# Fourier position transform split into even and odd parts, in a two-layer diffusion backbone on one core

## The reference, cut to what matters

```python
def fourier_mix(u, w_four):
    bn, length = u.shape[:2]
    ug = u.astype(jnp.float32).reshape(bn, length, C_GROUPS, C_GROUP_DIM)
    f = jnp.fft.fft2(ug, axes=(1, 3), norm='ortho').real.astype(u.dtype)
    return jnp.einsum('blgc,gcd->blgd', f, w_four).reshape(bn, length, C_WIDTH)

o = jnp.concatenate([window_attention_latent(...), global_attention_latent(...),
                     fourier_mix(uf, p['w_four'])], axis=-1) @ p['w_out']
h = h + g2 * o
```

## Time and profile before

| | us |
|---|---|
| median of 3 runs | 2835.33 |
| the profiled execution, as timed | 2834.34 |
| its span, first to last instruction | 2832.6 |
| PE busy | 2723.1 (96%) |
| DVE busy | 1471.4 (52%) |
| ACT busy | 981.8 (35%) |
| POOL busy | 767.5 (27%) |

### The profile page before, as it was taken

How to read it: one execution, slowest core, us unless ns; L and a number is a source line. 1 busy time by engine, 2 the same in 40 slices (tenths; PEclk the granted TensorE clock), 3 DMA queues, 4 the chain that set the end, 5 groups by cost and what they waited for, 6 DMA issues and landing times.

```text
span 2832.6 us, 37039 instructions
## 1 busy us (share of the span) xinstructions
PE 2723.1 (96%) x15204; PEld 2325.5 (82%) x15204; DVE 1471.4 (52%) x1926; ACT 981.8 (35%) x1503; POOL 767.5 (27%) x570
## 2 busy tenths in 40 slices
PE   6999999999988999999999999999999998999998
PEld 2888888888776888888888888888887777888887
DVE  1656655645288455565552555654225477433333
ACT  2433233324267243333331433332223366422232
POOL 1223422323167312343221132431011256100001
PEclk8999999999999999999999999999999999999999
DMA  5333333313411123333321233332212520233232
GB/s 222 101 108 124 120 103 112 111 54 138 134 36 37 38 100 109 113 127 106 113 91 60 86 113 123 126 97 78 68 59 94 160 60 1 82 97 104 89 99 81
DMA packets 70584, 274.36 MB, mean 97 GB/s; under 512 B 8720, under 2 KB 12048, under 8 KB 69392
## 3 DMA queue, kind: packets, MB, share of 16 engines
q1 hardware_dynamic: 70416, 271.99, 30.0%
HBM read 258.85 MB, written 13.11 MB: 96 GB/s over the span
## 4 chain that ended last, share of the span: by engine, by line
PE 84%; POOL 6%; DVE 4%; issue 2%; ACT 2%; DMA 1%; SPq 1%; POOLq 0%; DVEq 0%; ACTq 0%
PE ring L1337 72%; PE ring L1346 6%; POOL prob L518 4%; PE row L1187 1%; DVE wlo L932 1%; POOL xl L506 1%; PE ring L1296 1%; PE row L1444 1%; DMA q<-qk_parts 1%; ACT whi L609 1%; DVE t L1025 1%; DVE xl L1031 1%; PE row L1261 0%; PE bank L1422 0%; POOL xh L502 0%
## 5 line engine op out<-in xcount | busy, mean ns | idle before, releaser
L1337 PE MATMUL ring<-xh,whi 128*128 128x512 f32 (+1 forms) x2712 | 754.0, 346 | 10.6 <-DVE wlo L932 7.0
L1337 PE MATMUL ring<-xh,wlo 128*128 128x512 f32 (+1 forms) x2712 | 750.4, 345 | 0.0
L1337 PE MATMUL ring<-xl,whi 128*128 128x512 f32 (+1 forms) x2712 | 750.3, 345 | 0.0
L932 DVE TENSOR_TENSOR wlo<-raw,whi 128x1024 fp32r<-128x1024 f32 (+1 forms) x280 | 389.5, 1391 | 507.1 <-ACT whi L609 506.5
L462 POOL TENSOR_TENSOR ada_acc<-ada_acc,ada_tmp 128x384 f32<-128x384 f32 x252 | 335.2, 1330 | 601.7 <-ACT ada_tmp L621 581.0
L1337 PEld LDWEIGHTS ring<-xh,whi 128*128 128x128 f32 x2712 | 428.5, 188 | 77.1 <-issue 8.6
L1337 PEld LDWEIGHTS ring<-xh,wlo 128*128 128x128 f32 x2712 | 428.8, 188 | 66.2
L1337 PEld LDWEIGHTS ring<-xl,whi 128*128 128x128 f32 x2712 | 428.5, 188 | 65.4
L609 ACT ACTIVATE whi<-raw 128x1024 fp32r<-128x1024 f32 (+1 forms) x280 | 314.5, 1123 | 195.2 <-PE ring L1337 185.7
L949 DVE SCALAR_TENSOR_TENSOR ada_acc<-ada_buf,scond,ada_acc 128x384 f32<-128x384 f32 x294 | 353.6, 1203 | 6.9
L1337 PE MATMUL ring<-ah,whi 128*128 128x512 f32 (+1 forms) x1078 | 299.3, 347 | 0.0
(11 more groups left out here) (152 smaller groups left out, 2990.5 us busy)
## 6 DMA issues: line engine op xcount, KB each, us to landing
raw<-w_gu SPq DMA_DIRECT2D x176, 512.0 KB, 3.5
ada_buf<-w_ada SPq DMA_DIRECT2D x84, 768.0 KB, 4.2
raw<-w_down SPq DMA_DIRECT2D x64, 704.0 KB, 4.0
raw<-w_in SPq DMA_DIRECT2D x24, 512.0 KB, 3.6
ada_first<-w_ada SPq DMA_DIRECT2D x6, 1536.0 KB, 10.5
raw<-w_out SPq DMA_DIRECT2D x16, 512.0 KB, 3.7
k<-qk_parts SPq DMA_DIRECT2D x16, 384.0 KB, 6.7
q<-qk_parts SPq DMA_DIRECT2D x8, 576.0 KB, 9.8
```

The lines of the kernel that those rows point to most:

```text
L932: dve.tensor_tensor(wlo[:, slot, 0:nk * P], raw[:, slot, 0:nk * P], whi[:, slot, 0:nk * P].bitcast(F32), ALU.subtract).then_inc(wlo_ready, 1)
L1337: last = pe.matmul(out[:, a:b], w, x[:, k, a:b], start=(i == 0 and m == 0), stop=(i == nk - 1 and m == 2))
```

## The change

The position tables hold, per token block, 257 (129) cosine columns and 256 (128) sine columns, instead of 512 (256) of each. The cosine products go to one bank and the sine products to another. Chunk 0 uses `row[:, 0:512]` and `row[:, 512:1024]`; chunk 1 uses `row[:, 1024:1536]` and `bank[0]`, so it waits for nothing of chunk 0. ACT copies the odd part to `fodd` in SBUF. DVE forms the first half as even + odd, copies the middle column, and writes the second half mirrored as even - odd, into `fsum` in SBUF. ACT then rounds `fsum` into `xh` and DVE subtracts into `xl`. The transposes of tile 0 wait for `fsum_done` of chunk 1. The split of the second `w_out` tile moves from step 5 to the place behind the copies of `v1`. The rounding of chunk 1 moves to step 4 on ACT, and its rest to step 5 on DVE. The first write of ACT into the second half of `pth`, which lies over `fsum`, waits for that rest.

```diff
+        def fourier_banks(c):
+            return (row[:, 0:512], row[:, 512:1024]) if c == 0 else (row[:, 1024:1536], bank[0])
...
-        def act_fourier(act, layer):
+        def act_fourier(act, layer, between):
...
             for c in range(2):
                 wd = w_in_width(layer, UF[0])
+                odd, wo = fourier_banks(c)[1], (SEQ + CTX) // 2 if wd == TOK else SEQ // 2
+                if c == 0:
+                    between()
                 act.wait_ge(f2_done, 2 * layer + c + 1)
-                act.activation(xh[:, 6 + c, 0:wd], side[:, 0:wd], ACT.Copy).then_inc(fhi_done, 1)
+                act.activation(fodd[:, c, 0:wo], odd[:, 0:wo], ACT.Copy).then_inc(fodd_done, 1)
+                if c == 0:
+                    round_fourier(act, layer, 0)
+
+        def round_fourier(act, layer, c):
+            wd = w_in_width(layer, UF[0])
+            act.wait_ge(fsum_done, 2 * layer + c + 1)
+            act.activation(xh[:, 6 + c, 0:wd], fsum[:, c, 0:wd], ACT.Copy).then_inc(fhi_done, 1)
...
                         if i == 2:
-                            act_fourier(act, layer)
-                        if i == 5:
-                            split_hi(t + W_IN_TILES + 1, 1, KD)
+                            act_fourier(act, layer, lambda: split_hi(t + W_IN_TILES + 1, 1, KD))
+                        if i == 4:
+                            round_fourier(act, layer, 1)
...
+                            if j == 3:
+                                act.wait_ge(flo_done, 2 * layer + 2)
...
+            between()
             for c in range(2):
                 wd = w_in_width(layer, UF[0])
-                dve.wait_ge(fhi_done, 2 * layer + c + 1)
-                dve.tensor_tensor(xl[:, 6 + c, 0:wd], side[:, 0:wd], xh[:, 6 + c, 0:wd].bitcast(F32), ALU.subtract).then_inc(flo_done, 1)
+                dve.wait_ge(fodd_done, 2 * layer + c + 1)
+                even = fourier_banks(c)[0]
+                for n_, o, e0, o0 in ((SEQ, 0, 0, 0), (CTX, SEQ, SEQ // 2 + 1, SEQ // 2))[:2 if wd == TOK else 1]:
+                    hn = n_ // 2
+                    dve.tensor_tensor(fsum[:, c, o:o + hn], even[:, e0:e0 + hn], fodd[:, c, o0:o0 + hn], ALU.add)
+                    dve.tensor_copy(fsum[:, c, o + hn:o + hn + 1], even[:, e0 + hn:e0 + hn + 1])
+                    last = dve.tensor_tensor(fsum[:, c, o + n_ - 1:o + hn:-1], even[:, e0 + 1:e0 + hn], fodd[:, c, o0 + 1:o0 + hn], ALU.subtract)
+                last.then_inc(fsum_done, 1)
+                if c == 0:
+                    rest_of_fourier(dve, layer, 0)
...
                 if i == 2:
-                    dve_fourier(dve, layer)
+                    dve_fourier(dve, layer, lambda: split_lo(s["t"] + W_IN_TILES + 1, 1, KD))
                 if i == 5:
-                    split_lo(s["t"] + W_IN_TILES + 1, 1, KD)
+                    rest_of_fourier(dve, layer, 1)
...
-                    if c == 1:
-                        pe.wait_ge(flo_done, 2 * layer + 1)
-                    for tab, b0, nb, (lo, hi) in ((pos_lat, 0, 4, (0, SEQ)), (pos_ctx, 4, 2, (SEQ, TOK)))[:2 if blocks == 6 else 1]:
+                    even, odd = fourier_banks(c)
+                    for tab, n_, b0, e0, o0 in ((pos_lat, SEQ, 0, 0, 0), (pos_ctx, CTX, 4, SEQ // 2 + 1, SEQ // 2))[:2 if blocks == 6 else 1]:
+                        nb, hn = n_ // P, n_ // 2
                         for m in range(nb):
-                            for part in range(2):
-                                last = pe.matmul(side[:, lo:hi], v1[:, b0 + m, c, part * P:(part + 1) * P], tab[:, part, m],
-                                                 start=(m == 0 and part == 0), stop=(m == nb - 1 and part == 1))
+                            pe.matmul(even[:, e0:e0 + hn + 1], v1[:, b0 + m, c, 0:P], tab[:, m, 0:hn + 1], start=(m == 0), stop=(m == nb - 1))
+                        for m in range(nb):
+                            last = pe.matmul(odd[:, o0:o0 + hn], v1[:, b0 + m, c, P:2 * P], tab[:, m, hn + 1:n_ + 1], start=(m == 0), stop=(m == nb - 1))
...
-                    pe.wait_ge(flo_done, 2 * layer + 2)
+                    pe.wait_ge(fsum_done, 2 * layer + 2)
```

More of the change, by code:

```diff
@@ L226, in build @@
         uf = sb("uf", [P, 2, TOK], F32, work + 49152)
-        pos_lat = sb("pos_lat", [P, 2, 4, SEQ], F32, work + 55296)
-        pos_ctx = sb("pos_ctx", [P, 2, 2, CTX], F32, work + 71680)
+        pos_lat = sb("pos_lat", [P, 4, SEQ + 1], F32, work + 55296)
+        pos_ctx = sb("pos_ctx", [P, 2, CTX + 1], F32, work + 63520)
+        fsum = sb("fsum", [P, 2, TOK], F32, work + 65600)
+        fodd = sb("fodd", [P, 2, TOK // 2], F32, work + 71744)
         v1 = sb("v1", [P, 6, 2, 2 * P], F32, work + 75776)
@@ L274, in build @@
         f1_done, v1_even, v1_odd = sem("f1_done"), sem("v1_even"), sem("v1_odd")
-        f2_done = sem("f2_done")
+        f2_done, fodd_done, fsum_done = sem("f2_done"), sem("fodd_done"), sem("fsum_done")
         bn_done, bstd_done, brstd_done, unorm_done = sem("bn_done"), sem("bstd_done"), sem("brstd_done"), sem("unorm_done")
@@ L867, in dve_w_in, with dve_fourier @@
             rest_values(1)
-        def dve_fourier(dve, layer):
+        def dve_fourier(dve, layer, between):
             for blk in (1, 3, 5):
@@ L873, in dve_fourier, with rest_of_fourier @@
                 dve.tensor_copy(v1[:, blk].rearrange("p c n -> p (c n)"), bank[1][:, 0:4 * P]).then_inc(v1_odd, 1)
+            between()
             for c in range(2):
                 wd = w_in_width(layer, UF[0])
-                dve.wait_ge(fhi_done, 2 * layer + c + 1)
-                dve.tensor_tensor(xl[:, 6 + c, 0:wd], side[:, 0:wd], xh[:, 6 + c, 0:wd].bitcast(F32), ALU.subtract).then_inc(flo_done, 1)
+                dve.wait_ge(fodd_done, 2 * layer + c + 1)
[8 more added lines that the diff above has]
+                    rest_of_fourier(dve, layer, 0)
+        def rest_of_fourier(dve, layer, c):
+            wd = w_in_width(layer, UF[0])
+            dve.wait_ge(fhi_done, 2 * layer + c + 1)
+            dve.tensor_tensor(xl[:, 6 + c, 0:wd], fsum[:, c, 0:wd], xh[:, 6 + c, 0:wd].bitcast(F32), ALU.subtract).then_inc(flo_done, 1)
         def dve_attention(dve, s, split_lo):
@@ L1539, in positions @@
         cos, sin = dft(n)
-        return np.stack([cos, -sin]).reshape(2, n // P, P, n).transpose(2, 0, 1, 3)
+        return np.concatenate([cos[:, :n // 2 + 1], -sin[:, :n // 2]], 1).reshape(n // P, P, n + 1).transpose(1, 0, 2)
     f = lambda a: np.ascontiguousarray(a, dtype=np.float32)
```

## The result

The changed kernel takes 2806.91 us (median of 4 runs, 2804.24 to 2811.22), beside 2835.8 for the kernel before in the same job (4 runs, 2834.63 to 2840.38). The ratio is 0.9899 with a 95% interval of 0.9884 to 0.9913, a gain of 28.9 us. A second job gave 2807.6 against 2835.18 (15 runs of the kernel before), ratio 0.9904, 0.989 to 0.9917, so 27.2 us with bounds of 23.5 and 31.2. The forecast was 2811.3 with a range of 2808 to 2818. The time lies 1.1 us under the range. The two profiled executions, 2834.34 and 2807.93, differ by 26.4 us, where 24.0 was forecast.

What follows compares the result with a forecast made beforehand. PE, busy 96% of the span, was taken as the bound. Products 18.6, opening 0.6, step 5 2.2 and clock 3.6 make 25.0 us, less 1.0 for POOL waits: 24.0 us, forecast 2811.3 us, range 2808 to 2818.

Steps and rivals of the forecast that it cites:

- Products, 18.6 us: Products over positions: halved columns and no wait between chunks save 10.4 us in the first layer, 8.2 in the second.
- Cover of the weight tile's split: First layer: weight tile's rounding and subtraction end at 763.9, before chunk 0 ends on PE at 764.7, covered by 0.8 us.
- The prediction's second case: Weight load 2 us later: chunk 0's ACT and DVE work moves 1.2 us, ends at 768.3, before chunk 1 at 769.1.
- Opening, 0.6: Opening of the attention: tile 2's exponential follows the first scores sooner, gaining 0.1 us in the first layer, 0.5 in the second.
- Step 5, 2.2: Step 5 of the attention: without the weight tile's split PE restarts 1.0 us sooner in one layer, 1.2 in the other.
- The clock, 3.6, and 5.2 us from restart to tile 9: Behind step 5's pauses: clock stays up, restart to tile 9's scores takes 5.2 us, saving 1.1 + 2.5 us.
- deduction of 1.0 us: Taken off the summed gain of 25.0 us, for tiles that come sooner and wait for POOL at some places.
- part 4: The clock behind step 5's pauses staying up: 3.6 us gained, bounds 0 and 5.1.
- parts 1 to 3: Products 18.6 us (18.2 to 18.9), opening 0.6 (loss of 0.4 to gain of 0.9), step 5 2.2 (1 to 3.8).
- A: Rival: the half clock stays behind the shorter pauses in both layers; 2814.3 us, chance 0.25.
- B: Rival: opening bound by POOL and the DVE-ACT exchange, so only the products' gain is left; 2817.3 us, chance 0.15.
- C and D: Rivals: C, passes don't shrink, 2834 us, chance 0.02; D, clock drops from the products' start, slower, 2850 us, chance 0.03.

Runs made afterwards that it cites:

- banks_only: The kernel before with separate banks for chunk 1 and no wait between the chunks, full columns; 2827.26 us, ratio 0.9972.
- same_banks: The changed kernel with both chunks in chunk 0's banks, so chunk 1's products wait for chunk 0's sum; halved columns; 2813.55 us.
- double: The changed kernel with every product over positions issued twice into the same accumulation; 2825.22 us.
- split_back: The changed kernel with the second output weight tile's split put back into step 5; 2813.34 us.
- again: The changed kernel run once more with no edit; 2807.6 us.
- full_load: The changed kernel with two more loads, so as many bytes come with the position tables as before; 2807.29 us.
- before_again: The kernel before run once more for a second trace, no edit; 2833.48 us.
- the two POOL kernels: The changed kernel with chunk 1's rounding and rest moved to POOL (2806.94 us), or only the rest, a subtraction (2806.24 us).
- split_only: The kernel before with only the second output weight tile's split moved from step 5 to behind the copies of v1; 2826.61 us, ratio 0.9973.

## Why the prediction was wrong, and where it was right

*Products, 18.6 us.* Right: 10.5 + 8.3 = 18.8. Passes of 256 columns stand (1.89 - 0.38)/7 = 0.216 apart. `banks_only` and `same_banks` split it: the waits between chunks are worth 3.8 either way, the halved columns 15.0. In `double` the added products cost the mixers their own time (15.6 and 15.3).

*Cover of the weight tile's split.* Right, and roomier than reckoned (1.8 us instead of 0.8), because this load landed earlier. The prediction's second case has a slip: had chunk 0's work moved by 1.2 us, it would have ended at 764.7 + 1.2 + 3.6 = 769.5, behind the products' end at 769.1 and not covered. It did not come to that.

*Opening, 0.6.* Nearly: 2.71 and 2256.65 - 2254.39 = 2.26 us, a gain of 0.1 and 0.3. The unknown price of the mirrored write is nothing.

*Step 5, 2.2.* Right: 1.90 to 0.74 and 1.91 to 0.57, 2.5 us.

*The clock, 3.6, and 5.2 us from restart to tile 9.* Right for this kernel: 5.20 us in both layers, so 1.15 + 2.53 = 3.7, and no half clock in the openings of any kernel whose pause had gone. The reason I gave was too simple. With the pause at 1.9 us, `banks_only` shows full clock in one layer and short half clock in the other, so the pause makes the half clock likely and does not set its length. The Trainium skill (TensorE: Matmul & The Clock Gate, HAM oscillation) has waits of PE drop the clock; the kernel before and `split_back` agree (0.57 and 0.79), the first layer of `banks_only` (1.00) and the earlier trace rows do not.

*The deduction of 1.0 us, "tiles that come sooner will at some places wait for POOL".* This is the step that failed. It measured nothing. PE's waits for POOL in the first and in the second attention, kernel before and then changed kernel (us in total, times, longest us):

```profile
PE row L1261 <- POOL prob L518: 9.5, 11, 2.2
PE row L1261 <- POOL prob L518: 4.4, 8, 1.6
```

```profile
PE row L1295 <- POOL prob L524: 9.3, 10, 2.2
PE row L1295 <- POOL prob L524: 4.4, 8, 1.6
```

PE does not wait longer for POOL than before, although the tiles come sooner. The mixers went from 338.5 us (mean of two traces) to 313.7 (mean of the changed kernel, `again` and `full_load`): 24.8 us, against 25.0 before the deduction.

*From the sum to the time.* The forecast of 2811.3 is 4.4 us too high, and the traces divide that in three. The mixers of the two profiled executions differ by 338.65 - 313.90 = 24.75 us, where 24.0 was forecast: 0.75, the deduction less the 0.25 by which the other terms were too high. The two executions differ by 26.4, so 1.65 lies outside the edited places. And I put the median 1.0 above the profiled execution, as it was for the kernel before; for the changed kernel it was 1.0 below (2807.93 and 2806.91), which is 2.0. The second and the third belong to the level from which I counted: one execution, taken as if it repeated. `before_again` shows that it does not, since the wait of 1.23 us for q ahead of the first scores was in one trace and not in the other.

*The range.* Its lower end of 2808 took only two terms at their bounds (part 4 at 5.1, nothing given back: 2811.3 - 1.5 - 1.0 = 2808.8), although parts 1 to 3 had bounds of their own that reach, with these two, to 2806.6. It had nothing for the spread of executions.

*What the medians gained beyond the mixers.* The mixers give 24.8, the medians 27 to 29. The mean of the granted clock over all runs of the second job is 0.9884 for the kernel before (15 runs) and 0.9908 for the changed one (4 runs). That is 66 against 52 us at half clock, (1 - 0.9884)/0.5 x 2833 and (1 - 0.9908)/0.5 x 2806, so up to 7 us of time, of which the two openings hold 5.1. That would leave about 2 us for half clock at other places. But the four runs of the first job have a mean of 0.9900 and the larger gain, so the clock alone does not settle it. Half clock does lie at other places from execution to execution (in the kernel before, at 640 and 2152 us in the first trace alone, at 1581 in the second alone), and stretches of PE at full clock differ too (`again`). One program moved by 7 us in this way (2804.24 to 2811.22). Whether the changed kernel has less of it by design or by chance is not settled. The median less the mixers of the trace is 2493.0 to 2494.3 us in the changed kernel, `again`, `full_load` and the two POOL kernels, and 2495.1 in `before_again`. But it is 2495.0 to 2496.2 in `same_banks`, `split_back` and `double`, which have the change, and 2493.5 in `split_only`, which has full columns. So it does not go with the halved columns, and chance is the nearer reading. The interval of the second job (23.5 to 31.2 us) holds 24.8 as well.

Rivals A and B fell. A would have left 0.57 behind the restarts. B would have shown the scores of tile 9 earlier and the end of the attention not; counted from the first product they come 12.9 and 12.4 us earlier in `again`, and its mixers are 25.3 us shorter, which is all of it. C and D fell at once with 8.70 and 1.00.

## What to carry to other kernels

Where one engine is busy for 96% of a kernel, an fp32 product that can be cut by symmetry is worth its pass time in full, provided that no engine that combines the halves is needed elsewhere in that stretch; here ACT and DVE sat idle through it. Two long operations in a row, on two helper engines in the first steps of a pipelined loop, made PE wait 1.9 us, and the half clock that mostly followed cost about as much again (1.2 and 2.5 us). Moving them to a place where both helpers are idle was one edit of a few lines, and it was worth 5.4 us in the mixers (`split_only`). When a range is made, the spread of single executions belongs in it, not only the uncertainty of the terms.

## What the runs showed of the hardware that was not expected

The granted clock behind equal pauses of 1.9 us of PE was not equal. In us at half clock: 3.4 and 6.8 in the kernel before (0.57 over 4 and over 8 us), the same in its second trace, 3.4 twice in `split_back` (0.79 over 8 us), and none and 3.4 in `banks_only` (1.00 and 0.79). Behind pauses of 0.79 us or less none followed in sixteen openings. At a granted clock of 1.00 and PE busy throughout, one execution fitted 231 products into 40 us and another 235. A DVE write with a step of -1 over 255 fp32 columns took 0.41 us, as the plain one of 256 (0.42 to 0.43). POOL rounds 768 columns in 1.10 us and subtracts them in 1.82 to 2.09 us, where ACT and DVE need 0.84 and 0.96.
